# One-hot groups in pairs, the pair weights and x loaded earlier, and the selection at a new pace, in a two-block transformer kernel

## The reference, cut to what matters

```python
def block(hb):                                   # 128 tokens
    q = (hb @ wq).reshape(tc, PEER_HEADS, 2, PEER_HALF)
    s = jnp.einsum('thpk,hpnk->thpn', q, keys)   # 8 heads, 2 x 128 keys
    s_top, i_top = lax.top_k(s, PEER_TOPK)       # 16
    cand = s_top[:, :, 0, :, None] + s_top[:, :, 1, None, :]
    cid = i_top[:, :, 0, :, None] * N_KEYS + i_top[:, :, 1, None, :]
    best, pos = lax.top_k(cand.reshape(tc, PEER_HEADS, -1), PEER_TOPK)
    eid = jnp.take_along_axis(cid.reshape(tc, PEER_HEADS, -1), pos, -1)
    g = jax.nn.softmax(best.astype(jnp.float32), -1)
    act = jax.nn.gelu(jnp.einsum('td,thed->the', hb, u[eid]), approximate=False)
    return jnp.einsum('the,thed->td', g * act, v[eid])
```

## Time and profile before

| | us |
|---|---|
| median of 3 runs (lowest, highest) | 3786.34 (3786.01, 3790.39) |
| the profiled execution | 3789.86 |
| its span | 3787.8 |
| first pass, row 0 to the last table matmul | 494 to 1209 |
| TensorE idle between the passes | 1209.0 to 1232.3 |
| second pass | 1232.3 to 1791.1 |
| TensorE idle after it | 1791.1 to 1824.9 |

### The profile page before, as it was taken

One profiled execution on the slowest core, in us unless ns is written; L12 is line 12 of the kernel. 1 busy time (PEld: TensorE's weight loads), 2 busy tenths in 40 slices (PEclk: granted clock), 3 DMA queues, 4 the chain that ended last, 5 costly groups with the idle time before them and its releaser, 6 DMA issues. The chain is left out here.

```text
span 3787.8 us, 56067 instructions
## 1 busy us (share of the span) xinstructions
PE 3556.8 (94%) x21807; PEld 3153.1 (83%) x21807; DVE 2732.2 (72%) x5456; ACT 1689.3 (45%) x3029; POOL 395.3 (10%) x282
## 2 busy tenths in 40 slices
PE   7999999999997999998699999999997899989899
PEld 5777998999897877887577999998886888988798
DVE  4557366878786888888546797778887767766775
ACT  4344233555554333333434444443334535564554
POOL 0000000000454343343200000000000000000000
PEclk9999999999999999999899999999998999999999
DMA  5133366544899999998213575556665213442243
GB/s 229 63 132 133 114 244 253 186 168 167 324 352 346 332 390 365 369 381 310 85 51 145 184 231 186 167 184 229 251 242 187 112 72 146 181 169 90 83 173 139
DMA packets 181767, 773.02 MB, mean 204 GB/s; under 512 B 22976, under 2 KB 70592, under 8 KB 131584
## 3 DMA queue, kind: packets, MB, share of 16 engines
q1 hardware_dynamic: 144640, 635.20, 46.3%
q0 software_dynamic: 36864, 134.23, 9.4%
HBM read 699.38 MB, written 69.99 MB: 203 GB/s over the span
## 5 line engine op out<-in xcount | busy, mean ns | idle before, releaser
L2907 DVE TENSOR_TENSOR expert_ring_low<-expert_ring,expert_high 128x1024 fp32r<-128x1024 f32 x256 | 312.9, 1222 | 169.9 <-ACT expert_high L3236 166.6
L2192 ACT ACTIVATE expert_high<-expert_ring 128x1024 fp32r<-128x1024 f32 x256 | 270.6, 1057 | 211.3 <-PE ps L2119 211.3
L1922 DVE TENSOR_TENSOR expert_ring_low<-expert_ring,expert_high 128x1024 fp32r<-128x1024 f32 x256 | 311.7, 1219 | 70.7 <-ACT expert_high L2192 70.7
L3133 PE MATMUL ps<-hidden_high,expert_high 128*128 128x384 f32 x1024 | 353.7, 345 | 0.0
L3135 PE MATMUL ps<-hidden_high,expert_ring_low 128*128 128x384 f32 x1024 | 344.2, 336 | 0.0
L3134 PE MATMUL ps<-hidden_low,expert_high 128*128 128x384 f32 x1024 | 343.8, 336 | 0.0
L3236 ACT ACTIVATE expert_high<-expert_ring 128x1024 fp32r<-128x1024 f32 x256 | 270.0, 1055 | 118.0 <-PE ps L3170 112.5
L3424 POOL DMA_INDIRECT x<-in_peer_rows,spots x128 | 181.4, 1417 | 1107.7 <-DVE spots L2979 605.0
L2088 PE MATMUL ps<-peer_hT_high_peer,expert_high 128*128 128x256 f32 x1024 | 293.9, 287 | 0.6 <-DVE expert_ring_low L1922 0.5
L2090 PE MATMUL ps<-peer_hT_high_peer,expert_ring_low 128*128 128x256 f32 x1024 | 287.0, 280 | 0.0
L2089 PE MATMUL ps<-peer_hT_low,expert_high 128*128 128x256 f32 x1024 | 287.0, 280 | 0.0
(11 more groups left out here) (777 smaller groups left out, 9762.4 us busy)
## 6 DMA issues: line engine op xcount, KB each, us to landing
expert_ring<-in_peer_u SPq DMA_DIRECT2D x128, 1024.0 KB
expert_ring<-in_peer_v SPq DMA_DIRECT2D x128, 1024.0 KB
weight_ring<-in_ffn_w_up SPq DMA_DIRECT2D x22, 2048.0 KB, 7.5
weight_ring<-in_w_in SPq DMA_DIRECT2D x14, 2048.0 KB, 7.3
weight_ring<-in_w_mod SPq DMA_DIRECT2D x12, 2048.0 KB, 7.5
mod_slot<-in_w_mod SPq DMA_DIRECT2D x12, 2048.0 KB, 10.5
pair_weights<-pair_weights_out SPq DMA_DIRECT2D x24, 1024.0 KB
gelu_first<-gelu_out SPq DMA_DIRECT2D x62, 384.0 KB
```

Source lines behind the costliest of these rows:

```text
L1922: dve.tensor_tensor(piece(low, n), piece(raw, n), high[:, n % LEAD, :].bitcast(F32), ALU.subtract).then_inc(low_done, 1)
L2192: act.activation(high[:, n % LEAD, :], piece(raw, n), ACT.Identity).then_inc(high_done, 1)
L2907: dve.tensor_tensor(self.piece(G.e_low, n), self.piece(G.e_raw, n), G.e_high[:, n % LEAD, :].bitcast(F32), ALU.subtract).then_inc(self.S.l ...
L3133: pe.matmul(o, b[:, s], B.hs[0][:, c, 0:DW], start=(c == 0), stop=False)
```

## The change

- 20 key rows of gelu are kept in SBUF (`STAY`): the last 16 in a new buffer `gelu_kept`, four in the ring. The second pass begins with key row 108 instead of 124, and four stores' and loads' worth of rows no longer go through DRAM.
- `w_in` moves to the place of the table's buffers, which are dead by then; `gelu_kept` takes the place that it had.
- Ten of the table rows (98, 100, ... 116) do two groups, so the last group is in row 117 instead of 127, and the last rows of the pass have none. The budget of such a row for other pieces is less by 1250.
- The first loads of gelu and of pair weights are issued in row 124 instead of behind the pass.
- `EARLY_NS` goes from 2600 to 3900 and `TABLE_NS` from 2300 to 3300.
- ScalarE does `high_weights` of the first two rows ahead of the last gelu, and TensorE's first `products_v` takes the token tiles in the order 1, 2, 0, so that it needs the last gelu only for tile 0.
- `x_last` and `x` are loaded when row 124 of the second pass is done, ahead of the weights.

```diff
@@ -2849,7 +2849,8 @@
 PARTS = PAIRS // PART
 LAG = PART + 2
 U_SLOTS, V_SLOTS = 3, 4
-EARLY_NS, TABLE_NS, DOWN_NS = 2600, 2300, 1700
+EARLY_NS, TABLE_NS, DOWN_NS = 3900, 3300, 1700
+STAY, RING = 20, 4
 GROW_AT = 40
 
 E_SIGNALS = (
@@ -2875,7 +2876,11 @@
 
     def expert(self, r):
 
-        return (r + N_KEYS - KEPT) % N_KEYS
+        return (r + N_KEYS - STAY) % N_KEYS
+
+    def gelu_at(self, e):
+
+        return self.B.ge_out[:, e % RING, :] if e < N_KEYS - STAY + RING else self.B.ge_kept[:, e - (N_KEYS - STAY + RING), :]
 
     def scores_of(self, g):
         k, n = divmod(4 * g, 2 * PEER_HEADS)
@@ -2885,6 +2890,10 @@
 
         return next((u for u in range(self.mod.hi) if 3 + 5 * u // 2 == r), None)
 
+    def tables_in(self, r):
+
+        return [g for g in range(TABLES) if TABLE_ROUND[g] == r]
+
     def weights_of(self, r):
 
         return (0, r) if r < KEPT else ((r + KEPT) // 8, (r + KEPT) % 8)
@@ -2895,6 +2904,8 @@
 
 
 SCORE_GROUPS = 4 * 2 * PEER_HEADS // 4
+DOUBLED = range(98, 118, 2)
+TABLE_ROUND = [r for r in range(TABLES_AT, N_KEYS) for _ in range(2 if r in DOUBLED else 1)][0:TABLES]
 W_LOADS = N_KEYS // 8 + 1
 
 
@@ -3044,8 +3055,8 @@
     def weigh(self, dve, r):
         S, B = self.S, self.B
         n, j = self.weights_of(r)
-        m = r // 4 - 1
-        if r < KEPT:
+        m = (r - STAY) // 4
+        if r < STAY:
             dve.wait_ge(S.gelu_done, self.expert(r) + 1)
         elif r % 4 == 0:
             dve.wait_ge(self.ge_landed[m % 2], 16 * (m // 2 + 1))
@@ -3053,7 +3064,7 @@
             dve.wait_ge(self.w_landed[n % 2], 16 * (n // 2 + 1))
         if r >= 1:
             dve.wait_ge(S.aw_split, r)
-        ge = B.ge_out[:, r, :] if r < KEPT else B.ge_in[:, m % 2, r % 4, :]
+        ge = self.gelu_at(self.expert(r)) if r < STAY else B.ge_in[:, m % 2, r % 4, :]
         w = B.w_in[:, n % 2, :, j * BLOCK:(j + 1) * BLOCK]
         dve.tensor_tensor(B.aw[:, :].rearrange("p (b t) -> p b t", t=BLOCK), ge.rearrange("p (b t) -> p b t", t=BLOCK), w,
                           ALU.mult).then_inc(S.aw_done, 1)
@@ -3079,12 +3090,13 @@
             at["now"] = r
             if r < N_KEYS - 1:
                 self.split_low(dve, r + LEAD)
-            if 0 <= r + 1 - TABLES_AT < TABLES:
-                self.equal(dve, r + 1 - TABLES_AT)
+            for g in self.tables_in(r + 1):
+                self.equal(dve, g)
+            left -= 1250 * max(0, len(self.tables_in(r + 1)) - 1)
             left += EARLY_NS if r < TABLES_AT - 1 else TABLE_NS
             while left > 0:
                 left -= next(pieces, left)
-        assert at["selected"] < N_KEYS - 8
+        assert at["selected"] < N_KEYS - STAY
         for r in range(2):
             self.weigh(dve, r)
             self.split_weights(dve, r)
@@ -3164,7 +3176,9 @@
         pe.wait_ge(S.aw_split, r + 1)
         pe.wait_ge(S.low_done, n + 1)
         v = (G.e_high[:, n % LEAD, :], self.piece(G.e_low, n))
-        for t in range(DT):
+        for t in (1, 2, 0):
+            if r == 0 and t == 0:
+                pe.wait_ge(S.gelu_done, N_KEYS)
             for x, y in PASSES:
                 for h in range(2):
                     mm = pe.matmul(G.ps[:, 2 * t + h, :], (B.ah, B.al)[x][:, r % 3, t * P:(t + 1) * P],
@@ -3211,9 +3225,9 @@
                     mod.sums(pe, u - 1, S.parts_out, S.sums_ready)
                 if u == mod.hi - 1:
                     mod.sums(pe, u, S.parts_out, S.sums_ready)
-            if r >= TABLES_AT:
-                self.table_of(pe, r - TABLES_AT)
-        pe.wait_ge(S.gelu_done, N_KEYS)
+            for g in self.tables_in(r):
+                self.table_of(pe, g)
+        pe.wait_ge(S.gelu_done, N_KEYS - 1)
         pe.wait_ge(S.w_out, TABLES)
         for r in range(N_KEYS):
             self.products_v(pe, r)
@@ -3238,9 +3252,9 @@
     def gelu(self, act, r):
         S, p = self.S, r // 2
         act.wait_ge(S.scored, r + 1)
-        if r % 2 == 0 and p >= 2:
+        if r % 2 == 0 and 2 <= p < (N_KEYS - STAY + RING) // 2:
             act.wait_ge(self.ge_stored[p % 2], 16 * (p // 2))
-        act.activation(self.B.ge_out[:, r % 4, :], self.G.ps[:, r % 3, 0:DW], ACT.Gelu).then_inc(S.gelu_done, 1)
+        act.activation(self.gelu_at(r), self.G.ps[:, r % 3, 0:DW], ACT.Gelu).then_inc(S.gelu_done, 1)
 
     def shares(self, act, g):
         S, B = self.S, self.B
@@ -3289,12 +3303,15 @@
             if n < LEAD:
                 self.split_high(act, n)
         for r in range(N_KEYS):
+            if r == N_KEYS - 1:
+                self.high_weights(act, 0)
+                self.high_weights(act, 1)
             self.gelu(act, r)
             if r in (0, 2):
                 keep_rows(r // 2)
             self.split_high(act, r + LEAD)
-            if 0 <= r + 1 - TABLES_AT < TABLES:
-                self.shares(act, r + 1 - TABLES_AT)
+            for g in self.tables_in(r + 1):
+                self.shares(act, g)
             for k in range(len(TILES)):
                 if r == at[f"shift{k}"]:
                     act.wait_ge(S.shift_ready, k + 1)
@@ -3304,12 +3321,10 @@
                 mod.part_out(act, u, S.parts_ready, S.parts_out, S.sums_ready)
                 if u == mod.hi - 1:
                     mod.out(act, S.sums_ready, S.mod_out)
-            if r > TABLES_AT:
-                self.table_out(act, r - TABLES_AT - 1)
+            for g in self.tables_in(r - 1):
+                self.table_out(act, g)
             self.gates(act, r)
-        self.table_out(act, TABLES - 1)
-        for r in range(3):
-            self.high_weights(act, r)
+        self.high_weights(act, 2)
         for r in range(N_KEYS):
             if N_KEYS + LEAD + r < N:
                 self.split_high(act, N_KEYS + LEAD + r)
@@ -3335,14 +3350,14 @@
     def load_ge(self, sp, m):
         B = self.B
         if m >= 2:
-            sp.wait_ge(self.S.aw_done, KEPT + 4 * (m - 1))
+            sp.wait_ge(self.S.aw_done, STAY + 4 * (m - 1))
         sp.dma_start(B.ge_in[:, m % 2, :, :], B.ge_dram[:, 4 * m:4 * m + 4, :]).then_inc(self.ge_landed[m % 2], 16)
 
     def load_w(self, sp, n):
         B = self.B
         if n >= 2:
             sp.wait_ge(self.S.aw_done, self.weights_end(n - 2))
-        first = (N_KEYS - KEPT, 0)[n > 0] if n == 0 else 8 * n - 8
+        first = self.expert(0 if n == 0 else self.weights_end(n - 1))
         size = 8 if 0 < n < W_LOADS - 1 else KEPT
         sp.dma_start(B.w_in[:, n % 2, :, 0:size * BLOCK],
                      B.w_dram[:, :, first * BLOCK:(first + size) * BLOCK].rearrange("b p n -> p b n")).then_inc(self.w_landed[n % 2], 16)
@@ -3356,7 +3371,7 @@
         for p in range(UNITS_U):
             sp.wait_ge(S.scored, UJ * (p + 1))
             self.load_unit(sp, p + E_SLOTS)
-            if UJ * p < N_KEYS - KEPT:
+            if UJ * p < N_KEYS - STAY:
                 sp.wait_ge(S.gelu_done, UJ * (p + 1))
                 sp.dma_start(B.ge_dram[:, UJ * p:UJ * p + UJ, :], B.ge_out[:, UJ * p % 4:UJ * p % 4 + UJ, :]).then_inc(
                     self.ge_stored[p % 2], 16)
@@ -3365,40 +3380,41 @@
                 if u is not None and u + 2 < mod.hi:
                     sp.wait_ge(S.parts_ready, u + 1)
                     mod.load(sp, u + 2, self.mod_landed)
-            while stored < BLOCKS and TABLES_AT + 4 * stored + 5 <= UJ * p + 1:
+            while stored < BLOCKS and TABLE_ROUND[4 * stored + 3] + 2 <= UJ * p + 1:
                 self.store_w(sp, stored)
                 stored += 1
-        for b in range(stored, BLOCKS):
-            self.store_w(sp, b)
-        sp.wait_ge(S.table_ready, DT)
-        for b in range(2):
-            sp.wait_ge(self.ge_stored[b], 16 * (N_KEYS - KEPT) // (2 * UJ))
-        self.load_ge(sp, 0)
-        self.load_ge(sp, 1)
-        for b in range(2):
-            sp.wait_ge(self.w_stored[b], 16 * BLOCKS // 2)
-        self.load_w(sp, 0)
-        self.load_w(sp, 1)
+            if p == UNITS_U - 2:
+                assert stored == BLOCKS
+                sp.wait_ge(S.table_ready, DT)
+                for b in range(2):
+                    sp.wait_ge(self.ge_stored[b], 16 * (N_KEYS - STAY) // (2 * UJ))
+                self.load_ge(sp, 0)
+                self.load_ge(sp, 1)
+                for b in range(2):
+                    sp.wait_ge(self.w_stored[b], 16 * BLOCKS // 2)
+                self.load_w(sp, 0)
+                self.load_w(sp, 1)
         for q in range(UNITS_U):
             r = UJ * (q + 1)
             sp.wait_ge(S.pv_done, r)
             if UNITS_U + q + E_SLOTS < 2 * UNITS_U:
                 self.load_unit(sp, UNITS_U + q + E_SLOTS)
-            if q % 2 == 1 and 2 <= q // 2 + 1 < (N_KEYS - KEPT) // 4:
-                self.load_ge(sp, q // 2 + 1)
+            if r % 4 == 0 and 2 <= (r - STAY) // 4 + 1 < (N_KEYS - STAY) // 4:
+                self.load_ge(sp, (r - STAY) // 4 + 1)
             n = (r - KEPT) // 8 + 2
             if r >= KEPT and (r - KEPT) % 8 == 0 and n < W_LOADS:
```

(10 more changed lines are left out.)

## The result

The changed kernel takes 3800.4 us (median of 6 runs, 3797.2 to 3808.3) against 3785.8 of the kernel before (6 runs, 3782.8 to 3790.4): ratio 1.0039, 95% interval 1.0028 to 1.0050. It is slower; 3775 and "faster" were forecast. The profiled span is 3795.4 (before 3787.8).

What follows compares the result with a forecast made beforehand. TensorE bounds the stage, and a ring through ScalarE and VectorE sets first-pass table rows at 5.51 us. 34 - 12 - 17 - 16 = -11 gave 3778.9 profiled, less 3.5 to the median: 3775 us, range 3750 to 3806.

Steps and rivals of the forecast that it cites:

- First pass: First pass over the key rows: all its terms together lengthen it by 34 us, ending at about 1243 instead of 1209.
- doubled groups: Ten table rows: a second group adds 1.67 us each, ten last rows without one save 13.4; net +3 us.
- pieces: VectorE's dots, sums and selection work in table rows: beyond 3.23 us they lengthen the row, +17 us.
- exponentials: Softmax switches of ScalarE's function table: two instead of three such rows fall among the table rows, -3 us.
- gates: ScalarE's waits for the eighth dot of a part, stretching the ring in table rows: +5 us, bounds 0 and 20.
- the gathers' traffic: First pass: +5 us for late gathers at their start, +7 for fuller DMA in rows 55 to 97.
- Hole between the passes: TensorE's stop between the passes: early pair-weight loads shrink it from 23.3 to 11.5 us, -12, bounds -17 and -3.
- Rival 3: Between the passes: early pair weights stuck behind gathers and gelu, hole near 20, 3784 us; chance 0.12.
- Second pass: Second pass: sums end in row 52, fewer stalls and less lower clock behind it, -17 us, bounds -8 and -26.
- Hole behind: TensorE's stop behind the second pass: x loaded earlier lands in time, -16 us, bounds -16 and -12.
- Rival 4: Rows 55 to 97: transfers limited near 358 GB/s, a row of 6.6 us, 3796 us; chance 0.06.
- Rival 2: Rows 55 to 97: gathers set the first pass, 6.85 us a row on average, 3806 us; chance 0.17.

Runs made afterwards that it cites:

- e1: Changed kernel with the old pace of VectorE's pieces (EARLY_NS 2600, TABLE_NS 2300): 3785.5 us, ratio 0.9992 to the kernel before.
- e5: Changed kernel without the gathers' transfers but the first few, same dots and sums, results left wrong: 3745.9 us, ratio 0.9889 to the kernel before.
- e3: Changed kernel with no pieces of VectorE's selection or sparse tile in rows 116 to 127: 3777.5 us, ratio 0.9966 to the kernel before.
- e6: Changed kernel with the two early pair-weight loads issued ahead of the two early gelu loads: 3795.1 us, ratio 1.0014 to the kernel before.
- e4: Kernel before with only the load of x moved to row 124 of the second pass, ahead of the weights: 3771.3 us, ratio 0.9947.
- e2: Kernel before with only the new pace (EARLY_NS 3900, TABLE_NS 3300): 3826.1 us, ratio 1.0094.
- e9: Kernel before with only EARLY_NS at 3900, TABLE_NS left at 2300: 3775.0 us, ratio 0.9969.
- e7: Changed kernel with pair weights ahead of gelu, TABLE_NS back at 2300, no pieces from row 120 on: 3742.0 us, ratio 0.9881 to the kernel before.
- e8: Changed kernel with pair weights ahead of gelu, TABLE_NS 2600, no pieces from row 118 on: 3753.6 us, ratio 0.9908 to the kernel before.

## Why the prediction was wrong

By its own terms (predicted, measured; us):

- **First pass**, +34, +41.5. e1 gives the doubled groups as they were priced (+3, measured +2.0), so the pace cost 39.5 where the sum had 31. What e5 leaves (its pieces, doubled groups, exponentials, gates: 17 - 3 + 3 + 5 = 22) measured 14.8; the gathers' traffic (5 + 7 = 12) measured 26.7. A comparison of sizes, since the kernel before has traffic of its own in it. By place the pass grew 9.8 us in rows 32 to 54, where the prediction's tally of selection pieces and exponentials comes to some 2 and no gather runs; 19.1 in rows 55 to 96; and 12.8 from row 97 on, where it had the doubled groups' 3 and let all of VectorE's lag be paid in the hole. Rows 55 to 96 lasted 6.20 on average (gelu of row 55 at 810.2, of row 97 at 1070.5), predicted 6.08; but they are not even: rows 55 to 60, where the gathers start, took 41.8 us against 33.1, and of the 36 behind them 14 are at the ring's 5.51 (before 31) and one reaches 9.1. The ten doubled rows lasted 7.33 on average, 1.82 above 5.51, predicted 1.67; a plain row (5.51) and a doubled one (7.25) from the timeline of ScalarE:

```profile
1077.51 0.47 ACT L3257 ACTIVATE gelu_out<-ps 128x384 f32<-128x384 f32 x1
1083.02 0.47 ACT L3257 ACTIVATE gelu_out<-ps 128x384 f32<-128x384 f32 x1
1090.27 0.47 ACT L3257 ACTIVATE gelu_out<-ps 128x384 f32<-128x384 f32 x1
```

- **Hole between the passes**, -12, +4.0. *This is the step that failed*, by 16 of the 21 us between -11 and +10, and with the sign. It took the 9.5 us of a load from a stretch in which these loads had 90% of the engines' time into one that the same change had filled with gathers, and let it land 12 to 18 us after row 125; and it let VectorE do its last five pieces in 5.9 us. Measured: 32.8 for the load at 40% of the engines' time, and eight pieces and a split done 16.7 us after TensorE stopped. Rival 3 named the place and the cause (stuck behind gathers and gelu, hole near 20) and got 0.12; even it was too mild. e3 (6.3) and e5 (9.9) show the cause, e6 that the gelu loads ahead had a share.
- **Second pass**, -17, -20.3: right. The two stalls of 4.0 and 2.2 that are left lie in its first 160 us, and behind 1500 the clock is 1.00 and TensorE never idle, as said.
- **Hole behind**, -16, -15.2: right, and confirmed alone by e4.
- **Rival 4**, a limit near 358 GB/s: the 390 over 160 us go against it. The Trainium skill itself says so on another page: "Perfetto Trace Analysis" (Roofline) has one active core pull more than 358, up to about 435. This trace agrees. **Rival 2** (gathers set the first pass) was to decide from 6.3 us a row; at 6.20 it nearly did.

What the sum got wrong in kind is that it priced the early load in the surroundings of the kernel before. The pace fills the transfers and the early load needs them free, both in rows 117 to 127: the early load takes 6.4 us off the hole on the old pace (e1) and nothing on the new one (27.3 in e2 as in the changed kernel). This meeting turned the forecast gain of the hole into a loss. It is not why the kernel is slower at all: the pace in table rows costs more alone (e2, +0.94%) than in the change. The parts that pay are the faster pace where no table group runs (-0.31%, e9), the early x (-0.4 to -0.5%, e4) and, with quiet rows, the early load (21 us of hole, e7).

Open: how the 26.7 us of traffic divide between late dots, late expert units and the lower clock of 0.95; the runs take them away together. Open too is what it would be without the gathers' traffic in the kernel before; no such run was made.

## What to carry to other kernels

A load's latency belongs to the traffic it was measured in: before moving a load earlier, read the DMA share of the place where it will then lie, and thin out what else moves there. Pull work forward only up to the room that the bounding ring leaves it (here 3.2 us of VectorE a row): below that edge it is free, and a nominal budget that now and then lets in one piece too many cost 12 us over the pass (e8). Price a part of a change by a run of that part alone before adding it to a sum: the pace alone showed the loss at once. When a change has several parts, look for a pair that wants the same resource in the same rows.

## What the runs showed of the hardware

- From the issue of the two pair-weight loads on SyncE to VectorE's use of the first: 9.5 us in the kernel before, when only the last gathers were still landing, 8.2 (e7, no gelu loads ahead) and 11.2 (e3, two of them ahead) with gathers stopped, 21.9 with 1.84 gathers a row (e1), 24.9 (e6, none ahead) and 32.8 (changed, two ahead) with 2.64. In all six VectorE was waiting for the load. The gathers are issued by GpSimd on a queue of their own and slow SyncE's loads all the same: their queue had 64% of the engines' time in the changed kernel, the loads' 40%, against 19% and 90% before. The Trainium skill, "DMA: Bandwidth & Descriptors" (Issuing engines are not separate DMA queues), says that DMAs of all issuing engines end on the same 16 DMA engines and interleave; these times agree.
- SyncE itself is held by the issue of these loads: 7.0 us before, 8.5 in e3, 21.0 in the changed kernel, and the next expert unit, whose row was scored by 1250.5, goes out behind it at 1264.09.
- The share of the transfers went above 1 at fewer bytes: 1.09 at 318 GB/s between issue and use of the pair-weight loads in the kernel before (109% by the two queues above), 1.07 at 370 in the changed kernel's hole and 1.19 at 291 in that of e5, against 1.01 at 390 over the 160 us with expert units, stores and gathers. A share is time of the engines, not bytes.
